# One layer of a hybrid streaming encoder: the stores of the weight sums move from the load queue to ScalarE

## The reference

```
n = RMSNorm(x)
h = x + W_out( sig(g_pool) * PoolBranch(n) + sig(g_attn) * W_attn_up(SWA(n)) )
h = h + W_down( relu(RMSNorm(h) W_up)^2 )          # W_up 1024 x 4096, W_down 4096 x 1024
y = RMSNorm_final(h)
```

## Time and profile before

| | |
|---|---|
| median of 3 runs | 2495.96 us (2495.28 to 2500.68) |
| profiled execution, time | 2496.72 us |
| profiled execution, span | 2494.9 us |
| mean granted clock of TensorE | 0.985 |
| TensorE busy | 2366.1 us, 95% of the span |
| VectorE busy | 1674.4 us, 67% |
| ScalarE busy | 1162.6 us, 47% |
| GpSimd busy | 354.1 us, 14% |
| DMA of SyncE's queue | 336.08 MB, 42.9% of 16 engines' span |
| DMA of ScalarE's queue | 8.75 MB, 0.9% |

### The profile page before, as it was taken

One profiled execution on the slowest core, in us unless ns is written; L12 is line 12 of the kernel. 1 busy time (PEld: TensorE's weight loads), 2 busy tenths in 40 slices (PEclk: granted clock), 3 DMA queues, 4 the chain that ended last, 5 costly groups with the idle time before them and its releaser, 6 DMA issues.

```text
span 2494.9 us, 41589 instructions
## 1 busy us (share of the span) xinstructions
PE 2366.1 (95%) x16389; PEld 2185.7 (88%) x16389; DVE 1674.4 (67%) x2592; ACT 1162.6 (47%) x2082; POOL 354.1 (14%) x296
## 2 busy tenths in 40 slices
PE   8999998888889998999999999999999999899997
PEld 8999998888877787999998787899998777799997
DVE  7655633232467557987797556987888656778877
ACT  4533422121334435665563434665664433656653
POOL 1400333333353100000003300000002400000000
PEclk9999999999999999999999999999999999999998
DMA  4222444444443234655653232666554223465563
GB/s 160 74 77 98 141 150 148 136 139 150 147 156 119 71 102 131 198 173 181 183 166 127 65 96 93 198 182 182 178 162 161 80 83 99 137 183 178 172 185 112
DMA packets 146289, 347.49 MB, mean 139 GB/s; under 512 B 17200, under 2 KB 17552, under 8 KB 142000
## 3 DMA queue, kind: packets, MB, share of 16 engines
q1 hardware_dynamic: 141360, 336.08, 42.9%
q10 hardware_dynamic: 4736, 8.75, 0.9%
HBM read 302.47 MB, written 42.40 MB: 138 GB/s over the span
## 4 chain that ended last, share of the span: by engine, by line
PE 63%; DVE 10%; DMA 10%; POOL 7%; ACT 5%; issue 4%; SPq 1%; DVEq 0%; POOLq 0%; ACTq 0%
PE prod L484 30%; DMA weight_sums<-wsum 10%; PE auxB L700 6%; PE auxB L702 5%; PE auxB L701 5%; PE prod L700 4%; PE prod L702 4%; PE prod L701 4%; POOL wsum L1580 2%; DVE wring L1128 2%; POOL wsum L1582 2%; POOL wsum L1581 2%; POOL wsum L1583 2%; ACT wring L745 1%; DVE m7L L1128 1%
## 5 line engine op out<-in xcount | busy, mean ns | idle before, releaser
L484 PE MATMUL prod<-nH,wm 128*128 128x272 f32 (+1 forms) x3104 | 728.2, 335 | 36.2 <-DVE wm L1128 27.7
L484 PEld LDWEIGHTS prod<-nH,wm 128*128 128x128 f32 x3104 | 503.8, 191 | 99.2 <-issue 24.5
L745 ACT ACTIVATE wm<-raw 128x1024 fp32r<-128x1024 f32 x232 | 235.2, 1014 | 758.0 <-PE prod L484 475.3
L745 ACT ACTIVATE wring<-rawq 128x512 fp32r<-128x512 f32 x672 | 418.2, 628 | 241.7 <-PE auxB L702 132.1
L1128 DVE TENSOR_TENSOR wring<-rawq,wring 128x512 fp32r<-128x512 f32 x672 | 455.3, 685 | 60.3 <-PE prod L702 33.9
L484 PE MATMUL prod<-nL,wm 128*128 128x272 f32 (+1 forms) x1552 | 441.1, 333 | 0.0
L1128 DVE TENSOR_TENSOR wm<-raw,wm 128x1024 fp32r<-128x1024 f32 x232 | 287.0, 1237 | 222.9 <-ACT wm L745 222.1
L484 PE MATMUL prod<-midH,wm 128*128 128x272 f32 (+1 forms) x1664 | 345.1, 319 | 30.3 <-DVE wm L1128 23.7
L484 PEld LDWEIGHTS prod<-midH,wm 128*128 128x128 f32 x1664 | 260.0, 193 | 52.5 <-issue 27.0
L484 PEld LDWEIGHTS prod<-nL,wm 128*128 128x128 f32 x1552 | 266.0, 190 | 26.9 <-issue 0.5
L700 PE MATMUL auxB<-n7H,wring 128*128 128x256 f32 x768 | 221.6, 288 | 30.2 <-ACT zt L745 14.2
(11 more groups left out here) (171 smaller groups left out, 4429.6 us busy)
## 6 DMA issues: line engine op xcount, KB each, us to landing
raw<-weights SPq DMA_DIRECT2D x200, 512.0 KB, 3.5
rawq<-weight_sums SPq DMA_DIRECT2D x384, 256.0 KB, 3.5
rawq<-weights SPq DMA_DIRECT2D x288, 256.0 KB, 3.0
weight_sums<-wsum SPq DMA_DIRECT2D x32, 1024.0 KB, 8.0
raw<-weights SPq DMA_DIRECT2D x32, 320.0 KB, 2.8
y<-hT ACTq DMA_DIRECT2D x12, 512.0 KB, 2.9
xT<-x SPq DMA_DIRECT2D x16, 256.0 KB, 4.5
xT<-x SPq DMA_DIRECT2D x8, 272.0 KB, 5.2
```

Source lines behind the costliest of these rows:

```text
L484: ins = nc.tensor.matmul(out[:, s, 0:hi - lo], lhs, rhs[:, lo:hi], start=first, stop=last)
L745: return nc.scalar.activation(out, in_, ACT.Copy, scale=scale)
```

## The change

SyncE no longer issues any store of sums. ScalarE issues them: that of pair 0 after the square root at the start of block 0's MLP, that of pair p at the end of its step n = 2p-1. Each is preceded by a wait until GpSimd has summed the pair.

```diff
@@ SyncE
-            def store_sums(p):
-                wait(sp, s_S, p)
-                sp.dma_start(sums_d[p], wsum[p % 2][:, :, :]).then_inc(set_out[p % 2], 16)
...
                 if n == 3:
                     wait(sp, s_h, 0, KD - 1)
                     sp.dma_start(xT[:, :, 0:TB], x123[0, :, :, :]).then_inc(x_in, 16)
-                if n % 2 and n >= 7:
-                    store_sums((n - 7) // 2)
...
                     load_mixer_unit(b, i)
-                    if b == 1 and i in (1, 3, 5):
-                        store_sums(PHASES * PAIRS - 3 + i // 2)
@@ ScalarE
+            def store_sums(p):
+                wait(act, s_S, p)
+                act.dma_start(sums_d[p], wsum[p % 2][:, :, :]).then_inc(set_out[p % 2], 16)
+
+            def sums_step(n):
+                if n % 2 and n // 2 + 1 < PHASES * PAIRS:
+                    store_sums(n // 2 + 1)
...
                         square("x", 1, 2 * i - 8, xT)
                         square("x", 1, 2 * i - 7, xT)
+                    sums_step(n)
...
                         copy(hT[:, m, :], hT[:, m, :], g_fin[:, m:m + 1]).then_inc(s_fg.sem, 1)
+                    sums_step(n)
...
                     root("h", 0)
+                    store_sums(0)
```

## The result

The changed kernel takes 2420.2 us (median of 4 runs, 2419.6 to 2421.8), against 2498.3 us for the kernel before, run beside it (median of 4): ratio 0.9689, 95% interval 0.9672 to 0.9706. The forecast was 2419, with a range of 2411 to 2440. The profiled execution took 2420.7 us with a span of 2418.9 us, so 76.0 us of span are gone.

The account below looks back on a forecast made before the run. A ring of GpSimd's sums, their store and SyncE's order bounds block 0's MLP. From 2496.7 us, minus 64.7 (plain units) and 13.4 (start of block 1), plus 1, gives 2419.6, forecast 2419 us; range 2411 to 2440.

Parts of the forecast that it names:

- The ring and its pace: In block 0's MLP, GpSimd's sums and their store on SyncE never overlap: 14.97 us a pair against TensorE's 12.04.
- Term one: Plain units of block 0's MLP at TensorE's pace: unit 63 released at 650.6 instead of 715.31, gain 64.7 us.
- The start of block 1: From the last plain unit to the piece of 48 products: 125.5 us becomes 112.1, gain 13.4 us.
- The pace of the sums: Block 0's MLP: sums p end about 16.4 us after release 2p-5, leaving 25 us for a 3.5 us landing.
- The 1 us for small waits of VectorE: End of block 0, where reciprocal, rotation table and gained tiles crowd VectorE: an estimated loss of 1 us.
- The new wait on ScalarE costs nothing: ScalarE's wait for GpSimd's sums before each store in block 0's MLP: zero at steady pace.
- is the ring gone?: Block 0's MLP: landing plus sums, 14.2 us, at slowest 21.8, fits the 24.08 us before the buffer's next store.
- The rule on issuing engines: Rival: issuers share the DMA engines, so stores save only 13 us of issue, 2483 us, or nothing; chance 0.04.
- The slower rival: ScalarE waits for sums with splits behind it; slower from a store landing of 23.8 us, about 2529 us; chance 0.03.

Follow-up runs that it names:

- early, on SyncE: The kernel before, with each store one pair earlier in SyncE's order, right behind the two loads that waited for its sums: 2420.1 us, ratio 0.9685.
- store before loads: The kernel before, same SyncE queue and late condition, with only the order of the store and the two loads exchanged: 2420.6 us, ratio 0.9689.
- late, on ScalarE: The changed kernel with the old condition: ScalarE stores pair p only after pair p+1 is summed; 2421.6 us, ratio 0.9694.

## Why the prediction was right

**The ring and its pace.** Right: GpSimd, the store and SyncE's order set the pace of block 0's MLP, and without it TensorE runs at 6.03 us a unit (forecast 6.02), at a clock of 1.00. Term one came to 64.5 us of span (the last unit ended at 715.31 before; it is released at 650.85 now), forecast 64.7. Within it the pace of 6.02 lacked the 0.85 us of the sum of squares.

**The start of block 1.** From the release of the last plain unit to the piece of 48 products it is 112.1 us, as forecast to a tenth. Block 2 was a fair measure for block 1.

**The pace of the sums.** The prediction let the sums of pair p wait for a landed store and end 16.4 us after the release of unit 2p-5. They wait for raw weights instead, 29 times: for pair 6 they end at 326.64 (325.34 + 1.30), 13.5 us after the release of unit 7 at 313.17. The step had more slack than it was given.

**The 1 us for small waits of VectorE.** TensorE waited for nothing there. Instead 1.9 us went behind block 1, of which 1.6 between the pieces of block 2 and block 3. The trace shows one wait of ScalarE for a load of the stored sums, 1.6 us, that the trace before does not have. In four of the ten kernels above one of the two spacings between blocks 1, 2 and 3 is 586.0 to 586.2 us too, and 584.5 in nearly all the rest, but not always with such a wait: what lengthens a block now and then was not settled. That the total fits to 1.2 us is in part luck: the allowance of 1 us was not used where it was set, and stands in for time lost elsewhere.

**The new wait on ScalarE costs nothing.** Right; there is no such wait in the profile, and asking one pair earlier left the ratio where it was (0.9686 against 0.9689).

**What fed the gain, mis-sized.** The step "is the ring gone?" took a store's landing to be 8.0 us of its own and priced every case with it: landing plus sums 14.2 us against 24.08. The landing was 4.1 us, and 5.4 when the store was only taken out from behind the two loads on SyncE. The step itself holds with a long landing too, since two and three stores per pair cost nothing. But before the change the ring was not merely closed, it was closed and stretched by the loads between the wait and the store. Any one of three repairs brings all of the gain: open the ring (early, on SyncE), shorten it by order (store before loads), or by queue (late, on ScalarE). The change does the first and the third. The forecast named the first alone and was right on the time because one is enough; that a shorter landing alone would have brought the same was not in it.

**The rule on issuing engines.** The Trainium skill (DMA: Bandwidth & Descriptors, section "Issuing engines are not separate DMA queues") says that a second issuer saves only the time to issue. The gain of 78 us doesn't contradict it for the rate of the DMA engines, which was never short (a share of 0.45 in the earlier trace rows). The early store on SyncE, equally fast, shows that no second issuer is needed for the gain. But the late store on ScalarE gained as much with the old condition, by a landing of 6.2 instead of 8.0 us, and that is more than issue time. Here the measurement goes against the rule as it stands: on the other queue the store no longer stood behind the two loads.

**The slower rival.** Its price, a landing of 23.8 us, stayed out of reach: with three copies the slowest landing was 16.4 us. Its mechanism does exist, with ScalarE's wait two pairs further forward.

## What to carry to other kernels

A wait in a DMA queue's program delays every transfer behind it, and transfers between the wait and the one that others wait for are part of the ring too: put the store that frees a buffer first, ahead of the loads, or issue it from an engine that reaches that point when the data are made. Before crediting a new queue, try the same order on the old one. And compare a ring's turn with what the bounding engine needs for the same work: as long as the ring keeps that pace, but for a lag that the buffered units cover, even a closed ring with an engine waiting thirty times costs next to nothing.

## What the runs showed of the hardware

By the medians a store of 1 MB from SBUF to HBM took 4.1 us to land on a queue of its own in the changed kernel, 5.4 us on SyncE's queue ahead of the loads, 6.2 us when it went out on ScalarE's queue beside two fresh loads on SyncE's, and 6.5 and 8.0 us behind one or two loads of 0.5 MB in the same queue. With three stores of 1 MB and two loads of 0.5 MB in 12 us the core moved 356 GB/s at a DMA share of 0.92, both directions together, with no wait of TensorE. ScalarE issued such a store in 0.33 us while its own arithmetic went on; SyncE took 0.43 us right behind a load and 0.33 us ahead of the loads.
